# Near scores of a chunked recurrent mixer: copied under a mask instead of multiplied and summed

## The reference, cut to what matters

```python
# gated DeltaNet, one chunk
sol = lax.linalg.triangular_solve(eye + lmat, rhs, left_side=True, lower=True, unit_diagonal=True)
...
S_new = S * jnp.exp(gl)[..., None, None] + jnp.einsum('bhsk,bhsv->bhkv', kh * jnp.exp(gl[..., None] - g)[..., None], v_new)
...
# HGRN2, one chunk
attn = jnp.einsum('bthk,bshk,btshk->bhts', qc, kc, jnp.exp(diff))
o = jnp.einsum('bthk,bhkv->bthv', qc * jnp.exp(G), S) + jnp.einsum('bhts,bshv->bhtv', attn, vc)
S_new = jnp.exp(Gl)[..., None] * S + jnp.einsum('bshk,bshv->bhkv', kc * jnp.exp(Gl[:, None] - G), vc)
```

## Time and profile before

| | |
|---|---|
| time, median of 3 runs | 3712.78 us (3711.8 to 3724.65) |
| time of the profiled execution | 3712.64 us |
| its span, first to last instruction | 3710.7 us |
| busy in the span: PE, DVE, ACT, POOL | 90%, 49%, 38%, 11% |
| the stretch of the prompt mixers, 990 to 1780 us: PE, DVE, ACT, POOL busy | 687, 575, 366, 389 us |

### The profile page before, as it was taken

How to read it: one execution, slowest core, us unless ns; L and a number is a source line. 1 busy time by engine, 2 the same in 40 slices (tenths; PEclk the granted TensorE clock), 3 DMA queues, 4 the chain that set the end, 5 groups by cost and what they waited for, 6 DMA issues and landing times. The chain is left out here.

```text
span 3710.7 us, 52416 instructions
## 1 busy us (share of the span) xinstructions
PE 3327.3 (90%) x21605; PEld 3026.3 (82%) x21605; DVE 1830.2 (49%) x2434; ACT 1418.3 (38%) x2100; POOL 426.1 (11%) x450
## 2 busy tenths in 40 slices
PE   4899999996498888988359969999999999999998
PEld 3899999996388787888348859999999999999987
DVE  6233233222277777777446744454454454454465
ACT  6333323321244444443104533343343343343454
POOL 0000000000345555553300000000000000000000
PEclk6999999998689999999569979999999999999999
DMA  5223223223512222220225564334434444344353
GB/s 190 49 59 70 65 71 87 76 71 126 203 66 84 86 78 82 86 86 30 63 75 209 210 243 152 121 136 182 148 113 177 150 159 157 123 171 148 136 199 114
DMA packets 232372, 450.13 MB, mean 121 GB/s; under 512 B 41383, under 2 KB 115293, under 8 KB 228029
## 3 DMA queue, kind: packets, MB, share of 16 engines
q1 hardware_dynamic: 230020, 428.33, 34.2%
q10 hardware_dynamic: 2128, 18.56, 1.3%
HBM read 363.38 MB, written 83.47 MB: 120 GB/s over the span
## 5 line engine op out<-in xcount | busy, mean ns | idle before, releaser
L2762 PE MATMUL ff_p<-ff_h_hi,ff_w_hi 128*128 128x384 f32 (+1 forms) x1536 | 502.8, 327 | 24.9 <-DMA ff_h_lo<-tmp_h 24.9
L2764 PE MATMUL ff_p<-ff_h_hi,ff_w_lo 128*128 128x384 f32 (+1 forms) x1536 | 503.1, 328 | 0.0
L2763 PE MATMUL ff_p<-ff_h_lo,ff_w_hi 128*128 128x384 f32 (+1 forms) x1536 | 502.3, 327 | 0.0
L412 PE MATMUL pin_pz<-hi,pin_whi 128*128 128x424 f32 (+1 forms) x1320 | 469.1, 355 | 14.4 <-DVE pin_wlo L528 14.4
L413 PE MATMUL pin_pz<-lo,pin_whi 128*128 128x424 f32 (+1 forms) x1320 | 466.8, 354 | 0.0
L414 PE MATMUL pin_pz<-hi,pin_wlo 128*128 128x424 f32 (+1 forms) x1320 | 466.8, 354 | 0.0
L2781 PE MATMUL ff_p<-ff_w_lo,ff_f_hi 128*128 128x512 f32 (+1 forms) x1088 | 426.7, 392 | 0.0
L2782 PE MATMUL ff_p<-ff_w_hi,ff_f_lo 128*128 128x512 f32 (+1 forms) x1088 | 426.4, 392 | 0.0
L2780 PE MATMUL ff_p<-ff_w_hi,ff_f_hi 128*128 128x512 f32 (+1 forms) x1088 | 423.7, 389 | 0.0
L2865 DVE TENSOR_TENSOR ff_w_lo<-ff_w,ff_w_hi 128x1024 fp32r<-128x1024 f32 x192 | 235.2, 1225 | 346.1 <-ACT ff_w_hi L2813 346.1
L2813 ACT ACTIVATE ff_w_hi<-ff_w 128x1024 fp32r<-128x1024 f32 x192 | 203.6, 1060 | 389.0 <-PE ff_p L2782 384.6
(11 more groups left out here) (526 smaller groups left out, 5614.0 us busy)
## 6 DMA issues: line engine op xcount, KB each, us to landing
ff_w<-in_w_unit SPq DMA_DIRECT2D x192, 512.0 KB, 5.2
ff_w<-in_w_unit SPq DMA_DIRECT2D x48, 2048.0 KB, 8.0
tmp_z<-pin_z SPq DMA_DIRECT2D x32, 1024.0 KB, 5.2
mix_rb<-tmp_rows_p SPq DMA_DIRECT2D x16, 1152.0 KB, 5.7
pin_w<-in_w_in SPq DMA_DIRECT2D x33, 512.0 KB, 8.1
gat_wa<-in_w_ada ACTq DMA_DIRECT2D x8, 2048.0 KB, 29.2
mix_zb<-tmp_z SPq DMA_DIRECT2D x16, 640.0 KB, 4.4
tmp_h<-op_h_hi SPq DMA_DIRECT2D x17, 512.0 KB, 4.2
```

Of the source, the lines that this page charges most:

```text
L412: pe.matmul(pz[:, g, 0:n], whi[:, u, k], hi[:, k, at:at + n], start=(k == 0), stop=False)
L2762: pe.matmul(dst, w1_hi[:, u, k], hi, start=(k == 0), stop=False)
L2763: pe.matmul(dst, w1_hi[:, u, k], lo, start=False, stop=False)
L2764: mm = pe.matmul(dst, w1_lo[:, u, k], hi, start=False, stop=(k == KT - 1))
```

## The change

Three edits on DVE and two on their surroundings.

First, `mask` no longer multiplies. For each round it issues 14 predicated copies, one per level and head: 64 columns of PSUM are written into `near` where that level's mask is not zero. `near` is set to zero once before the tiles. Copies of one head wait for each other, those of the two heads alternate. `ph` and the sum over levels are gone; ACT's copy of `near` waits for the copies themselves and stands behind ACT's first copy of `x`.

Second, `rv` is made by six instructions, one per head, that multiply PSUM by a column of `cc` and add `bv`.

Third, the decays of `cm`, `gs` and `hs` as operations of their own are gone: where the new part is added from PSUM, one instruction per head pair decays the old state and adds. `dc` has three buffers instead of two, since the decays are now read later. The product `y_m` (L2302) moves behind the second `update`.

Last, `tiles` writes out all 17 bodies on ACT, POOL and DVE.

```diff
-            with eng.Fori(0, TILES // 2 - 2) as pair:
-                body(pair * 2 + 2, 0, pair + 1)
-                body(pair * 2 + 3, 1, pair + 1)
...
+            for t in range(TILES + 1):
+                body(t, t % 2, t // 2, first=(t == 0), last=(t >= TILES - 1), tail=(t == TILES))
...
                     for j, src in enumerate((pc, pd)):
                         act.wait_ge(S("round"), b(2, j + 1))
-                        act.wait_ge(S("masked"), b(2, j + 1))
+                        act.wait_ge(S("masked"), b(4, 2 * j + 2))
...
                     dve.wait_ge(S("round"), n)
-                    dve.tensor_tensor(ph[:, j:HH:2], src[:, :, 0:NEAR * CB].rearrange("p r (n c) -> p r n c", c=CB),
-                                      level_c[:].unsqueeze(1).broadcast_to([P, 2, NEAR, CB]), ALU.mult).then_inc(S("masked"), 1)
+                    if n > 2:
+                        dve.wait_ge(S("summed"), (n - 1) // 2)
+                        dve.wait_ge(S("masked"), 2 * n - 4)
+                    for l in range(NEAR):
+                        for par in range(2):
+                            if l:
+                                dve.wait_ge(picked[par], (n - 1) * (NEAR - 1) + l)
+                            ins = dve.copy_predicated(near[:, 2 * par + j], level_c[:, l, :].bitcast(mybir.dt.int32),
+                                                      src[:, par, l * CB:(l + 1) * CB])
...
-                    dve.wait_ge(S("masked"), b(2, 2))
-                    dve.tensor_reduce(near[:], ph[:].rearrange("p h n c -> p h c n"), AX.X, ALU.add).then_inc(S("near"), 1)
                     dve.wait_ge(S("ks"), b(1, 1))
-                    dve.tensor_tensor(hm(rv[:]), pv(pc, HD), colh(o, Q_NBEG, HD), ALU.mult).then_inc(S("rv"), 1)
+                    for h in range(MH):
+                        ins = dve.scalar_tensor_tensor(rv[:, h, :], pc[:, h // 3, (h % 3) * HD:(h % 3 + 1) * HD],
+                                                       cc[o][:, Q_NBEG, h:h + 1], bv[:, h, :], ALU.mult, ALU.add)
+                    ins.then_inc(S("rv"), 1)
...
-                    then(dve.tensor_tensor(cm[:], cm[:], dc[o][:, 0, :].unsqueeze(2).broadcast_to([P, 3, W]), ALU.mult))
-                    then(dve.tensor_tensor(gs[:], gs[:], dc[o][:, 1, :].unsqueeze(2).broadcast_to([P, 3, HD]), ALU.mult))
...
+                    for j in range(3):
+                        ins = dve.scalar_tensor_tensor(gs[:, j, :], gs[:, j, :], dl[:, 1, j:j + 1], pc[:, 0, j * HD:(j + 1) * HD],
+                                                       ALU.mult, ALU.add)
+                    ins.then_inc(S("gs"), 1)
```

More of the change, by code:

```diff
@@ L1676, in prompt_mixers @@
         rb, yt = two("rb", [P, MH, 3, P]), two("yt", [P, KT, P])
-        cc, dc, ex = two("cc", [P, NQ, MH]), two("dc", [P, 2, 3]), two("ex", [P, MH, 2, P])
+        cc, dc, ex = two("cc", [P, NQ, MH]), [sb(f"dc{k}", [P, 2, 3]) for k in range(3)], two("ex", [P, MH, 2, P])
         level = sb("level", [P, LEVELS + 1, P])
@@ L1707, in prompt_mixers @@
         za_in, zb_in, zg_in, rb_in, y_out = ([S(f"{n}{u}") for u in range(2)] for n in ("za_in", "zb_in", "zg_in", "rb_in", "y_out"))
+        picked = [S(f"picked{par}") for par in range(2)]
         CONSTS = 2
@@ L2028, in body @@
                     scores(pd, 1)
-            for t in range(TILES + 1):
-                body(t, t % 2, t // 2, first=(t == 0), last=(t >= TILES - 1), tail=(t == TILES))
+            tiles(body)
         @block.scalar
@@ L2078, in body @@
                     hgrn_decays(t)
+                if not tail:
+                    inverse(0)
                 if not first:
-                    act.wait_ge(S("near"), b(1, 1))
+                    act.wait_ge(S("masked"), b(4, 4))
                     for at in diagonal:
@@ L2083, in body @@
                     ins.then_inc(S("summed"), 1)
-                if not tail:
-                    inverse(0)
-                if not first:
                     act.wait_ge(S("xr"), b(1, 1))
@@ L2135, in body @@
                     act.activation(hm(xf[:]), pv(pb, P), ACT.Copy).then_inc(S("xf"), 1)
-            tiles(act, body)
+            tiles(body)
         @block.gpsimd
@@ L2194, in body @@
                     decays(t + 1, 1 - u)
-            tiles(pool, body)
+            tiles(body)
         @block.vector
@@ L2203, in _ @@
             dve.memset(ps[:], 0.0)
+            dve.memset(near[:], 0.0)
             dve.memset(den[:, 0, :], 0.0).then_inc(y_out[0], 16)
@@ L2319, in body @@
                     dve.tensor_tensor(yg, yg, six_of(pc, 1).rearrange("p (r j) c -> p r j c", r=2), ALU.add).then_inc(S("o_gdn"), 1)
-                    dve.tensor_tensor(hs[:], hs[:], pc[:, 1, MH * HD:512].rearrange("p (j c) -> p j c", j=2),
-                                      ALU.add).then_inc(S("hs"), 1)
+                    for j in range(2):
+                        ins = dve.scalar_tensor_tensor(hs[:, j, :], hs[:, j, :], eg[:, j, :], pc[:, 1, (MH + j) * HD:(MH + j + 1) * HD],
+                                                       ALU.mult, ALU.add)
+                    ins.then_inc(S("hs"), 1)
                 if not tail:
                     dve.wait_ge(S("e"), v(1, 1))
+                    if not first:
+                        dve.wait_ge(S("hs"), v(1, 1))
                     dve.tensor_copy(eg[:], e[:, LEVELS, :, P - 1:P])
@@ L2363, in body @@
                 dve.tensor_copy(den[:, 0, 2:3], den[:, 1, 2:3]).then_inc(S("step"), STEPS - count[0])
-            tiles(dve, body)
+            tiles(body)
             dve.wait_ge(S("gs"), TILES + 1)
```

41 lines of the change are left out of this document (18 added, 23 removed).

## The result

The changed kernel takes **3659.98 us** (median of 4 runs, 3649.81 to 3665.79); the kernel before took 3712.48 beside it. The ratio is 0.9846, 95% interval 0.9821 to 0.9871: faster by 1.5%, 52.5 us. Forecast were 3641 us in a range of 3628 to 3674. The profiled execution is the fastest of the four: 3649.81 us, span 3648.0.

The account below looks back on a forecast made before the run. PE's chain nearly sets the period, with waits for DVE's `rv` and `xt` and a low clock: 47.2 - 3.8 (waits) - 1.7 (clock) + 0.6 + 0.8 = 43.1 us per tile; 15 periods gain 70.5: 3641 us, range 3628 to 3674.

Parts of the forecast that it names:

- the change part by part: One tile laid anew from its second-round mask, each part of the change costed: 43.1 us per tile instead of 47.2.
- The copies: Head of the tile: 14 predicated copies at 0.133 us take 1.87 us, 0.87 more than before; PE's product starts 0.5 later.
- The sum and `rv`: At `solved`: the sum over levels leaves, six instructions of 0.15 us make `rv` before PE needs it; gain 1.54 us.
- The decays: At the first `update`: DVE is free when it is due, so `level_update(2)` starts 3.8 us earlier, both old waits included.
- The two new waits: PE waits 0.6 us for the second `update`, behind `decays` held by POOL's `hk`, and about 0.8 for the third.
- the clock: Behind PE's old wait at `level_update(2)`: full clock returns, gaining 1.7 us per tile.
- 43% of 4 us: Work lost to the low clock, mean 0.57, in 4 us behind the wait at 1247: 1.72 us.
- the sum: Total over tiles: 43.1 us per tile, 15 periods gain 70.5 us, longer tiles ending in the same order: 3641 us.
- No overlap: Rival, all short DVE instructions: each costs its whole duration, copies 0.21 us; 44.4 us per tile, 3660 us; chance 0.14.
- The clock keeps falling: Rival, PE: new waits bring the low clock on, the 1.7 us stay; 44.8 us per tile, 3667 us; chance 0.12.
- The copies become the bound: Rival, slower, head of the body: gain used up at 0.34 us per copy; at 0.40, 3737 us; chance 0.06.
- Nothing much: Rival, copies of 0.30 us: 46.6 us per tile; with waits bringing the low clock back, 3695 to 3715 us; chance 0.06.

Follow-up runs that it names:

- run 5: Run 1 with the copies of a round reordered, all seven of one head pair first, so each waits for the one just before: 3714.1 us, ratio 1.0016.
- Run 1: Changed kernel, with POOL made to wait for DVE's product of `y` ahead of the four operations that overtook it: 3644.4 us, ratio 0.9807.
- run 3: Kernel before with the predicated copies alone; `rv`, `y_m` and the three states as before: 3714.2 us, ratio 0.9998.
- run 9: Run 1 without the copies: product by masks and sum over levels are back, the sum behind `rv` and the product into `y`: 3648.9 us, ratio 0.9819.
- run 6: Run 1 with a second copy of same shape and source, into a spare tile without waits, ahead of every copy: 3751.6 us, ratio 1.0101.
- run 4: Changed kernel without the copies: product by masks, sum ahead of `rv`, ACT's copy of `near` ahead of its first `x`: 3666.9 us, ratio 0.9876.
- run 10: Run 1 with second update ahead of the decays and several DVE and ACT operations moved behind later updates or copies: 3690.0 us, ratio 0.9931.

## Why the prediction was right, and where it was off

**The tile** (*the change part by part*) came out at 43.2 to 43.4 where 43.1 was forecast. Counted from the start of the second-round mask, PE reaches these points after (us; measured from 1170.34, before from 1227.63):

| PE starts | before | forecast | measured |
|---|---|---|---|
| product with the identity (L1914) | 4.33 | 4.9 | 4.75 |
| `solved` | 7.90 | 6.37 | 6.03 |
| product behind the first update | 19.38 | 15.57 | 15.10 |
| behind the second | 24.74 | 19.82 | 20.02 |
| behind the third | 28.53 | 24.4 | 24.67 |

*The copies* were right to the digit, 0.133 us, and the 0.5 us by which the head is later nearly so (0.42). The path was right but not the only one: POOL's first `cl` ends at 1175.05, and the products from L1852 on, 0.33 later for the wait of 0.26, end with it at 1175.08. The forecast had only the first; that its number held is in part luck, and run 5 shows what the second costs when the copies are longer. By the Trainium skill, page "VectorE: DVE Perf Modes", section "The DRAIN you can't avoid", a next operation that is not held starts earlier than the drain of the one before would let it, which the prediction left out where it cites that section; 0.133 us between copies of 0.22 agrees. *The sum and `rv`*: 1.54 us were forecast, 1.87 gained, since the product ahead of `solved` starts 0.1 us sooner than forecast and lets `solved` start after 1.28 us instead of 1.46; the price of the six instructions was 0.19 each, not 0.15, and did not matter. *The decays*: 3.8 us forecast, 4.28 measured. The two new waits were forecast at 0.6 and 0.8 and are 0.52 and 0.51, for the reasons given. As a delay the second is larger than its wait: from the fourth point to the fifth PE takes 4.65 us, 0.86 more than before.

The term that was mis-sized is the clock, **1.7 us**. From the third point to the fourth PE took 5.36 us before and takes 4.92 now with a wait of 0.52, that is 4.40 of work, so the low clock had cost 0.96 there. In part, 43% of 4 us counted time as lost in which PE would have waited for ACT anyway; PE before, then now:

```profile
1248.28 1.37 PE L1838 MATMUL mix_pb<-mix_xt,mix_m 128*128 128x256 f32 x6
1249.45 1.61 PE L1838 MATMUL mix_pa<-mix_x,mix_cl 128*128 128x256 f32 x6
```

```profile
1186.72 0.87 PE L1832 MATMUL mix_pb<-mix_xt,mix_m 128*128 128x256 f32 x6
1187.87 0.95 PE L1832 MATMUL mix_pa<-mix_x,mix_cl 128*128 128x256 f32 x6 [0.28 <-ACT mix_x L2063]
```

The second of these starts 1.17 us after the first at the low clock and 1.15 at the high one. So the clock was set 0.7 too high and the gain from the two old waits 0.5 too low (3.8 for 4.28); that the tile came out within 0.3 us is owed in part to these two errors, which cancel.

**The missing 19 us** belong to no term of the tile. The step that failed is the last of *the sum*, which takes all 15 periods as equal. I had written that DVE work on two SBUF tensors stands still while POOL runs, and in the new tile applied it to `decays` alone; the product of `y` at L2350 is such work, beside POOL's differences and the four operations behind them. It never took over 1.67 us in the kernel before, where I looked:

```profile
L2343 DVE TENSOR_TENSOR mix_y<-mix_y,mix_ss x16: 1214/1406/1669, 1069.5 to 1771.8; 128x1024 f32<-128x1024 f32 x16
```

With the tile laid closer, it starts just ahead of the end of POOL's differences, where it came 0.7 us or more behind it before; there it wins, or loses and the tile is 4 us longer. Run 1 takes only this away: 3644.4 us, against 3641 plus 15 x 0.24 (43.34 instead of 43.1) = 3644.6.

**The rivals.** *No overlap* gave 3660 us, which is the measured median by chance: its copies of 0.21 are refuted by the row. *The clock keeps falling* is half right: in the two long tiles, behind a wait of 2.6 us that it did not foresee, and in one normal tile at no cost (0.96, 43.33 us). *The copies become the bound* had the right place, the head, though PE waits there at L1852 and not for `cl`, and the wrong price: the gain was to be used up at 0.34 us per copy, and run 5 shows it used up at 0.253 (1.0016 [0.9996, 1.0036]), even with POOL's wait. The sum behind 0.34 priced only PE's wait, not the clock that falls with it. The chance for slower, 0.06, was too small for that. *Nothing much* would have been right for the copies by themselves (run 3).

So the forecast was right in its places, and in its sum by errors that cancel; but a reader could take from it that the copies matter as much as the states, and the runs give them some 4 us of 70 where the sum stands behind `rv`.

## What to carry to other kernels

Where two engines take turns at one port, list every operation that can meet the other engine there, in the tile as it will be, not only those that wait now; a wait that sends the engine with time to spare behind the other took 15.6 us and most of the spread away. An operation of 3.4 us off the path costs hardly more than 0.9 us of work on it (0.46 us of PE's time in run 9, against 0.42 for the longer head): ask of each new instruction first whether it could stand elsewhere. And price a wait of PE together with the clock behind it, which in run 5 made 1.6 us more of wait into tiles 2 to 3.5 us longer.

## What was unexpected of the hardware

An operation of DVE that waits for POOL to end may miss its turn: the one at 1545.96 saw the last of the 14 differences end, and three small operations after it, without its turn, and ran only behind the fourth; the fifth was then held (2.67 us instead of 1.82). It need not miss it: `cc`, held from 1183.57, is done at 1186.95, just behind the end of `hk` at 1186.89, with POOL's next operation (L2181, from 1186.85) already there. The Trainium skill, page "SBUF — State Buffer", section "SBUF: two separate sides", has the port pair that DVE and GpSimd share, for a DVE operation with two SBUF inputs among others, as an exclusive lock for a whole instruction, which goes to the one that starts first. The rows agree that it is exclusive. They do not agree that the start decides, as recorded: DVE's product starts 0.2 us ahead of POOL's L2150 in the normal tile and in the long one alike. That the loser can lose four times in a row is what they add, 4.42 us for 1.3. Nor need the loser be large, or read two tensors: the second operation on `den`, one tensor of six columns, took 1.74 us (0.17 in the kernel before, at 1237.52), and `cc`, one of 48, took 3.38.

A wait on the copy just before nearly doubles the distance between copies, 0.253 us for 0.133 (run 5, where that copy also has the same source bank and output; the same source without the wait changes nothing, run 6).

Equal waits of PE had unequal prices. Behind 1.25 us (run 4) the clock fell in five tiles of 14; behind 0.97 and 1.12 close together (run 10) in seven; with waits of 0.5 (run 1) 13 tiles have a mean clock of 1.00, one 0.96, and that one is no longer than the others. What decides between equal tiles was not tried.
